# Five feed-forward stages with one plain tile ahead of the seven-product tiles where there were two, on one Trainium2 core

## The reference, cut to what matters

```python
def _swiglu(x, w_gate, w_up, w_down):
    return (jax.nn.silu(x @ w_gate) * (x @ w_up)) @ w_down

x = x + MACARON * _swiglu(_rmsnorm(x, ffn1_norm), ffn1_w_gate, ffn1_w_up, ffn1_w_down)
```

## Time and profile before

| | |
|---|---|
| median of 3 runs | 3106.76 us (3106.54 to 3106.76) |
| the profiled execution, its own time | 3106.85 us |
| its span, first to last instruction | 3105.6 us |
| granted TensorE clock, mean of the span | 0.999 |
| busy: PE, DVE, ACT, POOL | 3080.5, 2168.9, 1624.8, 1650.7 us |

### The profile page before, as it was taken

The page is one execution under the profiler, slowest core; times in us unless marked ns, Lnnn a source line. Parts: engine busy times, 40 slices in busy tenths (PEclk is TensorE's granted clock), DMA queues, the critical chain, the costliest instruction groups (busy, mean ns, idle before and its releaser), DMA issues. The chain is left out here.

```text
span 3105.6 us, 52754 instructions
## 1 busy us (share of the span) xinstructions
PE 3080.5 (99%) x20424; PEld 2827.1 (91%) x20424; DVE 2168.9 (70%) x2975; ACT 1624.8 (52%) x2567; POOL 1650.7 (53%) x994
## 2 busy tenths in 40 slices
PE   9999999999999999999999999999999999999999
PEld 8999888999989998888999877889999788889998
DVE  8776467877668774577877578558775786478773
ACT  6555433555556554335555455556554575455553
POOL 5676433677657675434767433226676112257674
PEclk9999999999999999999999999999999999999999
DMA  4323322232322232322223232322232223323232
GB/s 141 113 103 123 120 76 75 102 110 109 123 86 105 109 117 102 113 82 82 109 107 112 93 95 82 118 93 106 99 122 105 95 93 121 114 89 109 109 110 82
DMA packets 93320, 322.61 MB, mean 104 GB/s; under 512 B 10512, under 2 KB 14992, under 8 KB 93072
## 3 DMA queue, kind: packets, MB, share of 16 engines
q1 hardware_dynamic: 87680, 312.07, 28.5%
q10 hardware_dynamic: 5392, 7.17, 0.7%
HBM read 316.05 MB, written 2.10 MB: 102 GB/s over the span
## 5 line engine op out<-in xcount | busy, mean ns | idle before, releaser
L3121 POOL TENSOR_TENSOR wlo<-raws,whi 128x1024 fp32r<-128x1024 f32 x369 | 891.8, 2420 | 1135.8 <-ACT whi L1218 884.4
L1218 ACT ACTIVATE whi<-raws 128x1024 fp32r<-128x1024 f32 x422 | 441.0, 1051 | 159.2 <-PE bank L505 57.2
L3129 POOL TENSOR_TENSOR f_s<-f_s,R 128x512 f32<-128x512 f32 x132 | 172.4, 1306 | 193.8 <-ACT f_s L1308 192.4
L640 PE MATMUL bank<-gxh,whi 128*128 128x256 f32 x1064 | 268.8, 283 | 1.2 <-ACT acc L1364 1.2
L641 PE MATMUL bank<-gxl,whi 128*128 128x256 f32 x1064 | 268.6, 283 | 0.0
L2219 DVE TENSOR_TENSOR wlo<-banks,whi 128x1024 fp32r<-128x1024 f32 (+1 forms) x166 | 196.9, 1186 | 68.9 <-ACT whi L1335 68.9
L640 PE MATMUL bank<-f_th,f_sh 128*128 128x256 f32 x944 | 236.9, 283 | 0.0
L641 PE MATMUL bank<-f_tl,whi 128*128 128x256 f32 x944 | 236.7, 283 | 0.0
L640 PE MATMUL bank<-f_th,whi 128*128 128x256 f32 x944 | 236.7, 283 | 0.0
L641 PE MATMUL bank<-f_tl,f_sh 128*128 128x256 f32 x944 | 236.7, 283 | 0.0
L501 PE MATMUL bank<-gxh,whi 128*128 128x512 f32 x584 | 229.9, 394 | 1.4 <-DVE gxl L2161 1.4
(11 more groups left out here) (597 smaller groups left out, 9192.7 us busy)
## 6 DMA issues: line engine op xcount, KB each, us to landing
raws<-stream SPq DMA_DIRECT2D x588, 512.0 KB, 3.3
xa_mem<-memT ACTq DMA_DIRECT2D x2, 1024.0 KB, 6.2
m_dk<-decay ACTq DMA_DIRECT2D x2, 514.0 KB, 4.5
x<-xT ACTq DMA_DIRECT2D x4, 256.0 KB, 5.3
x<-xT SPq DMA_DIRECT2D x4, 256.0 KB, 6.6
outT<-x SPq DMA_DIRECT2D x2, 512.0 KB, 3.0
m_ct<-cos ACTq DMA_DIRECT2D x2, 256.0 KB, 2.6
m_sn<-sin ACTq DMA_DIRECT2D x2, 256.0 KB, 2.9
```

The costliest lines, as they stand in the source:

```text
L640: pe.matmul(out, seq(hi, k, P), moving[k][0], start=first and k == 0, stop=False, skip_group_check=n != 1)
L1218: act.activation(M.whi[r][:, :], M.raw[r][:, :], ACT.Copy).then_inc(*S.tick("hi", u))
L3121: pool.tensor_tensor(M.wlo[r][:, :], M.raw[r][:, :], M.whi[r][:, :].bitcast(F32), ALU.subtract).then_inc(*S.tick("lo", u))
L3129: pool.tensor_tensor(T["s"][:, :], T["s"][:, :], M.R[:, :], ALU.mult).then_inc(*S.tick("silu_scaled", f, m))
```

## The change

`PLAIN` becomes (4, 1, 1, 1, 1, 1). In the stages f = 1 to 5 hidden tile 1 is now a seven-product tile, item 0, and the seven-product tiles begin right behind tile 0. The start of these stages is written anew on three engines. TensorE's program is the same text. Stage f = 0 keeps its order. In the stream, the gate and up units of tile 1 have their rows blocked as in the later tiles.

On VectorE the order is now: `turn_lo`, a wait for `root(i)`, `sums(0)`, `s13_lo(0)`, `s24_lo(0)`, `rstd(i)`, `gate(0)`, `sums(1)`, `hidden(0)`, `s13_lo(1)`, `s24_lo(1)`, `turn_hidden(0)`, `first_row(0)`, and then `step(1)`, whose first instruction is `c22(0)`. The wait for `root` stands there because `sums` writes bank 7, which holds the norm's sum until the square root has read it.

```diff
-PLAIN = (4, 2, 2, 2, 2, 2)
+PLAIN = (4, 1, 1, 1, 1, 1)
...
+        def first_step():
+            snap(1, 0)
+            split_hi(rows(f, 1)[0])
+            snap(5, 0)
+            snap(6, 0)
+            silu(0)
+            s13_hi(1)
+            s24_hi(1)
+            m22_hi(1)
+            hidden_hi(0)
+            turned_hidden_hi(0)
...
         def begin(late):
-            split_hi(rows(f, 0)[0])
-            silu(late)
+            if f == 0:
+                split_hi(rows(f, 0)[0])
+                silu(late)
             s13_hi(0)
             s24_hi(0)
             m22_hi(0)
-            hidden_hi(late)
-            turned_hidden_hi(late)
+            if f == 0:
+                hidden_hi(late)
+                turned_hidden_hi(late)
 
         if f:
-            tile(0)
+            split_hi(rows(f, 0)[0])
             turn_hi(f, 3)
             root(i)
...
         begin(PLAIN[f] - 2)
-        for s in range(len(SEQS[f])):
+        if f:
+            first_step()
+        for s in range(1 if f else 0, len(SEQS[f])):
             step(s)
...
         if f:
             turn_lo(f, 3)
+            dve.wait_ge(*S.at("root", i))
+            sums(0)
+            s13_lo(0)
+            s24_lo(0)
             rstd(i)
+            gate(0)
+            sums(1)
+            hidden(0)
+            s13_lo(1)
+            s24_lo(1)
+            turn_hidden(0)
+            first_row(0)
...
-        gate(PLAIN[f] - 2)
-        begin(PLAIN[f] - 2)
-        for s in range(len(SEQS[f])):
+            gate(PLAIN[f] - 2)
+            begin(PLAIN[f] - 2)
+        for s in range(1 if f else 0, len(SEQS[f])):
             step(s)
...
         plain(0)
-        plain(1)
+        if f:
+            for u in rows(f, 0):
+                lo(u)
+            scale(0)
+        else:
+            plain(1)
...
-            if before[0] == "tile":
+            if before[0] == "tile" and before[1]:
                 scale(before[1])
```

More of the change, by code:

```diff
@@ L172, in turned_late @@
     m = (SEQS[f][s - 1] if s else ("tile", PLAIN[f] - 1))[1] if s >= 0 and (not s or SEQS[f][s - 1][0] == "tile") else 0
-    return m if m % 2 and m < PAIRED and m + 1 not in (F_PARTS[0][1], F_PARTS[1][1]) else 0
+    return m if m % 2 and m < PAIRED and m + 1 not in (F_PARTS[0][1], F_PARTS[1][1]) else None
 def freed(u):
@@ L1390, in step @@
                     turned_hidden_hi(before[1])
-        def tile(m):
-            ahead(("gate", f, m))
-            ahead(("up", f, m))
         def begin(late):
-            split_hi(rows(f, 0)[0])
-            silu(late)
+            if f == 0:
+                split_hi(rows(f, 0)[0])
+                silu(late)
             s13_hi(0)
```

## The result

The change makes the kernel slower. The median is 3130.25 us (3129.25 to 3131.81, four runs) against 3106.68 (3106.54 to 3106.76, four runs): a ratio of 1.0076, with a 95% interval of 1.0064 to 1.0089. The forecast was 3126.6 us, 3120 to 3132.5, and slower with a chance of 0.95. The difference is clear of the interval, but under 1%. The profiled execution took 3131.24 us, its span is 3129.7. The runs of this kernel fall into two groups 2 us apart (3129.25 and 3129.26; 3131.24 and 3131.81), which has to do with its last microseconds and is taken up at the end.

A forecast was written before the change was run, and what follows sets the result against it. TensorE, busy for 99% of the span, sets the time. Per stage 4.2 (up to c22(0)) + 0.5 (snapshot 5) - 0.80 saved gives 3.9 to 4.0; five stages add 19.75 us to 3106.85: 3126.6 us, range 3120 to 3132.5.

The forecast's parts named there:

- What is saved: Plain tile 1 as a seven-product tile costs 10.08 us instead of 10.88: 0.80 us saved a stage, 4.0 in five.
- (a): At each stage's start, product 5 of item 0 waits for s13_hi(0) and s13_lo(0); item 0 ends 0.95 us late.
- (b): Item 1 waits 2.6 us for GpSimd's low part of its up unit, queued behind scale(0).
- (c): Product 4 of item 0, issued within item 1, waits 0.6 us for c22(0) and starts at 587.0, 4.2 late.
- the chain is wrong: Sign: if the wait for c22(0) is missing or VectorE is idle in that stretch, VectorE's queue was misjudged.
- (d): Product 2 of item 1 waits 0.5 us (0.35 to 0.6) for snapshot 5, behind the late sums(2).
- From there on I find each thing ahead of its need: After snapshot 5 of item 1, no waits: snapshot 6 early by 0.4 us, snapshot 5 of item 2 by 0.3.
- rival 1: Further waits behind snapshot 5 of item 1: two more items lose 0.5 us each, 3131.6 us; chance 0.13.
- the one duration that varies: turn_hidden's L2296 on VectorE, 0.72 us or 1.37 beside GpSimd's work; taken as hindered, ending at 585.93.
- Rival 2: Only GpSimd's wait bites, VectorE's chain being shorter by 0.6 us or more: 2.75 us a stage, 3120.6; chance 0.07.
- Rival 3: TensorE's clock falls to half behind the wait for GpSimd's low part, losing 2.4 us a stage: 3138.6; chance 0.06.
- Rival 4: Not slower: TensorE's start has unseen slack, waits under 0.8 us a stage; with none, 3102.8 us; chance 0.05.

The follow-up runs named there:

- e1: The changed kernel with GpSimd making the low part of item 1's up unit ahead of scale(0), without waiting for item 1's sums; 3130.73 us.
- e6: The changed kernel with 18 unneeded matmuls ahead of the wait for GpSimd's low part in item 1 of the five stages; 3129.70 us.
- e13: The changed kernel with early norm sum, low part and c22(0), later tile 0 block sums, and ScalarE's snapshots mostly first in steps 1 to 7; 3128.28 us.
- e8: The changed kernel with silu(0) put back ahead of snapshot 1 of item 0 on ScalarE; 3146.74 us.
- e15: The changed kernel with early norm sum, low part and c22(0), reordered snapshots, and first_row(s) ahead of hidden in steps 2 to 7; 3119.26 us.
- e2: The changed kernel with first_row(0) and c22(0) ahead of s24_lo(1) and turn_hidden(0) on VectorE; 3128.55 us.
- e4: The changed kernel with the norm's matmuls ahead of tile 0's up unit and the square root ahead of turn_hi(f, 3); 3124.76 us.
- e5: The changed kernel with the reciprocal and gate(0) put back ahead of sums(0) on VectorE; 3152.48 us.
- e9: The changed kernel with the reciprocal on only 64 of 512 columns in the five stages, so not the full computation; 3122.60 us.
- e10: e9's short reciprocal, with silu(0) also put ahead of snapshot 6 of item 0 on ScalarE; 3118.03 us.

## Why the prediction was right, and where it was short

**What is saved.** 0.80 us a stage: right. Item 0 and the later ones run at 0.12 us a matmul.

**(a) Product 5 of item 0.** Forecast 0.95, measured 1.05. The difference is in the start-ups of 0.05 to 0.1 us behind each wait.

**(b) GpSimd's low part.** Forecast 2.6, measured 2.47. The unit did wait for `scale(0)`, the silu and the reciprocal. But e1 shows that this wait is no cause of the time: it can go, and nothing is gained, because (c) sets the same moment. The prediction says so ("VectorE's queue alone sets that").

**(c) `c22(0)`.** Forecast 0.6, and product 4 at 587.0, 4.2 late. In the changed kernel this wait isn't seen, since the clock's fall made TensorE arrive later by itself; product 4 started at 587.68, 5.1 late. In e6 with the full clock it starts at 587.00, and 571.27 + 11.52 = 582.79 was due: 4.21 late. By the prediction's own sign (no wait for `c22`: "the chain is wrong") the profile of the change alone would have spoken against it; it takes e6 to show the chain right.

**(d) Snapshot 5 of item 1.** Forecast 0.5. In e6 0.46 and a start-up of 0.10; in the changed kernel hidden like (c).

**"From there on I find each thing ahead of its need ... VectorE gains on TensorE with each item."** This is the step that failed, and it is where most of the missing time is. In e6 snapshot 5 of item 2 costs another 0.42 + 0.10 us, which is rival 1 in part (it supposed two more items of 0.5). Together e6 loses 4.21 + 0.56 + 0.52 = 5.29, with further start-ups 5.5, less 0.80 saved: 4.7 a stage, as its column "down" has it (4.68; 4.57 as the mean of the five), against 3.95 forecast. In the changed kernel the margin is gone as well: product 2 of item 2 starts at 600.72, 0.05 behind the end of that snapshot. VectorE hardly gains: its sums of tiles 3 to 8 are 4.81, 4.72, 4.70, 4.35, 4.35 and 4.36 us later than before (586.48 against 581.67, and so on to 637.70 against 633.34).

I had taken its idle time of 0.6 to 1 us in each tile for slack, and it is a wait inside its own loop. In an even tile it is the wait ahead of `hidden`. In an odd tile it was the 0.64 us ahead of `c22`, and the rows behind `hidden` show why that wait gave nothing back when it went. VectorE and GpSimd in the kernel before:

```profile
589.06 0.69 DVE L2286 TENSOR_TENSOR f_u<-bank,f_s 128x512 f32<-128x512 f32 x1 [0.98 <-POOL f_s L3129]
590.49 1.30 POOL L3134 TENSOR_TENSOR f_oddl<-f_u,f_oddh 128x512 fp32r<-128x512 f32 x1 [0.28 <-ACT f_oddh L1314]
591.34 0.73 DVE L2299 SCALAR_TENSOR_TENSOR xsd<-f_u,xsd 128x256 f32<-128x256 f32 x1
```

and in the changed one:

```profile
593.77 0.69 DVE L2298 TENSOR_TENSOR f_u<-bank,f_s 128x512 f32<-128x512 f32 x1 [0.98 <-POOL f_s L3152]
595.21 1.30 POOL L3157 TENSOR_TENSOR f_oddl<-f_u,f_oddh 128x512 fp32r<-128x512 f32 x1 [0.29 <-ACT f_oddh L1314]
595.40 1.38 DVE L2311 SCALAR_TENSOR_TENSOR xsd<-f_u,xsd 128x256 f32<-128x256 f32 x1
```

The first block sum of an odd tile (L2299, now L2311) starts 0.65 us sooner behind `hidden` and takes 1.38 us instead of 0.73: it ends 0.28 and 0.27 us behind GpSimd's low part either way. From the start of `hidden` to the next `sums` (592.66, 597.38) it is 3.60 us with the wait for TensorE and 3.61 without it. The same holds in 20 of the 35 odd tiles of the five stages in both kernels (0.27 to 0.29 us and 3.60 to 3.62 us). So the mis-sized term is this block sum, which the prediction took at its old length; it had called L2296 the one duration that varies. With 0.73 us the snapshot would have come at about 600.0 by my estimate, ahead of its need.

On TensorE the loss is there early: tile 3 begins 4.07 us late (594.86 against 590.79), tile 4 4.26 us (605.13 against 600.87), and at 4.26 it stays up to tile 8, with 0.09 more until the down projection. No later tile gives any of it back, and VectorE's queue ends up as late as TensorE. The "down" and "sums" columns of the table agree within 0.05 us in nine kernels of thirteen, over losses from 1.96 to 9.05 us. In e13 TensorE is 0.4 us later still because of the wait for `c22` behind tile 8. In e1 and e8 it is 0.2 and 0.55 us later. Both have a fall of the clock with no wait of TensorE behind it up to tile 8 that could cover it, which fits; no run has them with the full clock. In e15, where the loop was given slack, it is earlier.

**Rival 2** (only GpSimd's wait) is wrong: VectorE's chain was as long as added up. **Rival 3** (the clock) is right about the event and wrong about its price. The clock fell behind 2.6 us of standing, start to start, five times, and came back in the work behind it. The rule named there (the Trainium skill, TensorE: Matmul & The Clock Gate, part 1), that an idle TensorE is put down to half its clock and comes back after work, agrees with that in kind; e2 and e4 show that the same wait can also pass without a fall. And e6 shows the price in the changed kernel to be none, because the slowed matmuls filled waits that were due anyway. The prediction had argued from a longest other wait of 1.7 us that (b) would probably not be enough. **Rival 4** (not slower): `c22(0)` would have had to end by 583.6; it ended at 586.57.

**The sum.** 3126.6 forecast, 3130.25 measured, 3.65 us more. The five stages cost 22.54 us and not 19.75, which is 2.8 of it, the step above. The rest of about 1 us is the end of the program: the profiled execution ends with a window at half clock,

```profile
3120.50:3123.50 3.00, 2.93 (x13) 2.93 (x14) 1.39 (x5) 0.19 (x2) 0.00 (x0) 0.50 0.91 306
```

and from the last idle time of TensorE there (1.7 us, at L585) to the end it takes 1.8 us longer than the kernel before. Before, a window at the same place has a clock of 1.00, as it has in e6. That the runs of 3129.25 us are those without this fall fits the mean clocks (0.998 and 0.999 in them, 0.995 in the others), but only profiled executions show the place. This part isn't the change's doing. The kernel before has the same two groups, 3106.3 to 3106.9 and 3108.6 to 3109.1 us (27 and 11 of the 38 runs beside the experiments), but the four runs beside the changed kernel were all of the lower one. Like against like, the change costs 3129.25 - 3106.68 = 22.6 us. The forecast leaves this term out, and that its range held it is luck.

## What to carry to other kernels

When an engine's queue is delayed, ask what the loop costs that it is part of, and not how busy it is: an idle microsecond in which it waits for the consequence of its own earlier instruction is no slack. The longest wait in the list is then often the one that can be removed for nothing; the time is set by the last thing that the delayed queue delivers, here `c22` and snapshot 5 one item later. Idle time ahead of one instruction is no slack either if the next one lasts until another engine is done, as the block sum did. A delay can get lost again if the loop is given slack by its order, as in e15, though how much the one instruction moved into the gap gave isn't shown; and before a wait's clock penalty is added to a sum, look whether another wait ends behind it anyway.

## What the runs showed of the hardware that was not expected

- TensorE's clock fell to its lower level of 1.2 GHz (granted 0.50) behind waits of 2.31 us at five places of five in the change, behind the same waits (2.31 to 2.33 us) at four of five in e2, and behind 2.13 to 2.33 us at one of five in e4; behind 1.96 to 1.98 us at three of five in e1. So the length of the wait alone doesn't settle it. At the end of the program, behind the same 1.7 us of idle time at L585, it fell in the profiled executions of the change, e1 and e5 (the row of L585 takes 1.01 to 1.02 us there) and not in the others (0.60 to 0.61 us).
- In an odd tile VectorE's first block sum (L2299, L2311) ended 0.27 to 0.29 us behind GpSimd's L3134 (L3157) at 20 places in both kernels, whether it had started 0.45 us ahead of that end or up to 1.2 us.
- The silu begins 0.02 us behind its table load (577.16 + 1.28 and 578.46 in e9). The load's row is 1.28 us here as in the change, e8 and e10. The Trainium skill (ScalarE: Activation LUTs, What ACT_TABLE_LOAD costs) puts it at about 2.7 us with the drain; from the end of the snapshot ahead of it to the silu are 1.32 us here, so of the drain nothing is seen.
- Sums over 1024 columns on VectorE (L2219) took 1.52 us at 586.48, while GpSimd's L3167 ran until 586.92, and 1.22 at 597.38, where GpSimd stood still. In e2 the same sums began first (586.33, 1.22 us) and GpSimd's low part of the block sum (L3168, at 586.93) took 1.20 us and not 0.74.
